# Two groups of TensorE products in a linear attention layer, ordered by their contraction rows

## What is computed

```python
GLA_HEADS = 4; GLA_DK = 192; GLA_DV = 384; GLA_CHUNK = 16

def step(s, inp):                       # one chunk of the recurrence, all in float32
    qc, kc, vc, ac = inp
    bc = jnp.cumsum(ac, axis=2)         # the logarithm of the decay since the chunk's start
    o_inter = jnp.einsum('bhcd,bhde->bhce', qc * jnp.exp(bc), s)
    diff = bc[:, :, :, None, :] - bc[:, :, None, :, :]
    decay = jnp.exp(jnp.where(tril[:, :, None], diff, -jnp.inf))
    att = jnp.einsum('bhid,bhjd,bhijd->bhij', qc, kc, decay)
    o_intra = jnp.einsum('bhij,bhje->bhie', att, vc)
    last = bc[:, :, -1:, :]
    s_new = (jnp.exp(last[:, :, 0, :, None]) * s
             + jnp.einsum('bhcd,bhce->bhde', kc * jnp.exp(last - bc), vc))
    return s_new, o_inter + o_intra
```

## Time and profile before

| | us |
|---|---|
| median of 3 runs | 3801.09 |
| the 3 runs | 3800.23 to 3805.05 |
| the profiled execution, its own time | 3801.69 |
| its span in the trace | 3799.4 |
| PE busy | 3385.1 (89% of the span) |
| mean granted clock of TensorE | 0.909 of full speed |
| `score_levels`, from PE's first product to its last mask | 2479.1 to 2572.1 |
| the 8 sampled sequences of `linear_outputs` | 2601.6 to 2711.7 |

### The profile page before, as it was taken

How to read it: one execution, slowest core, us unless ns; L and a number is a source line. 1 busy time by engine, 2 the same in 40 slices (tenths; PEclk the granted TensorE clock), 3 DMA queues, 4 the chain that set the end, 5 groups by cost and what they waited for, 6 DMA issues and landing times. The chain is left out here.

```text
span 3799.4 us, 57145 instructions
## 1 busy us (share of the span) xinstructions
PE 3385.1 (89%) x23817; PEld 3082.7 (81%) x23817; DVE 1640.8 (43%) x1879; ACT 1274.2 (34%) x1363; POOL 208.7 (5%) x131
## 2 busy tenths in 40 slices
PE   7799999676567999999999999899659999999999
PEld 5699999354245999999999999763249999999999
DVE  4543334444554454333443444344444543334333
ACT  3432323123465343323333333230143433333322
POOL 0000000001231000000000000052010000000000
PEclk9899999656788999999999999957769999999999
DMA  4545352302564445454545444203235454445454
GB/s 145 184 159 174 118 158 86 122 1 89 178 200 134 156 156 166 145 166 157 165 155 165 153 161 166 74 1 128 88 140 166 147 163 154 164 158 164 146 166 136
DMA packets 317204, 537.06 MB, mean 141 GB/s; under 512 B 18213, under 2 KB 115455, under 8 KB 316040
## 3 DMA queue, kind: packets, MB, share of 16 engines
q1 hardware_dynamic: 316376, 529.70, 42.5%
q10 hardware_dynamic: 624, 4.46, 0.3%
HBM read 517.23 MB, written 25.19 MB: 143 GB/s over the span
## 5 line engine op out<-in xcount | busy, mean ns | idle before, releaser
L468 DVE TENSOR_TENSOR project_weights_low<-ring,project_weights_high 128x2048 fp32r<-128x2048 f32 x344 | 788.5, 2292 | 1201.9 <-ACT project_weights_high L403 1201.9
L403 ACT ACTIVATE project_weights_high<-ring 128x2048 fp32r<-128x2048 f32 x344 | 658.6, 1915 | 1263.3 <-PE project_banks L333 1263.2
L331 PE MATMUL project_banks<-high,project_weights_high 128*128 128x288 f32 x2560 | 763.9, 298 | 45.4 <-DVE project_weights_low L458 41.1
L332 PE MATMUL project_banks<-low,project_weights_high 128*128 128x288 f32 x2560 | 762.2, 298 | 0.0
L333 PE MATMUL project_banks<-high,project_weights_low 128*128 128x288 f32 x2560 | 761.8, 298 | 0.0
L331 PE MATMUL project_banks<-up_high,project_weights_high 128*128 128x288 f32 x2048 | 610.6, 298 | 27.5 <-DVE project_weights_low L458 27.5
L332 PE MATMUL project_banks<-up_low,project_weights_high 128*128 128x288 f32 x2048 | 609.6, 298 | 0.0
L333 PE MATMUL project_banks<-up_high,project_weights_low 128*128 128x288 f32 x2048 | 609.3, 298 | 0.0
L331 PEld LDWEIGHTS project_banks<-high,project_weights_high 128*128 128x128 f32 x2560 | 488.3, 191 | 48.1 <-DVE project_weights_low L458 42.6
L332 PEld LDWEIGHTS project_banks<-low,project_weights_high 128*128 128x128 f32 x2560 | 488.0, 191 | 0.0
L333 PEld LDWEIGHTS project_banks<-high,project_weights_low 128*128 128x128 f32 x2560 | 486.9, 190 | 0.0
(11 more groups left out here) (422 smaller groups left out, 3336.9 us busy)
## 6 DMA issues: line engine op xcount, KB each, us to landing
ring<-in_w_up_dram SPq DMA_DIRECT2D x128, 1024.0 KB, 5.2
ring<-in_w_down_dram SPq DMA_DIRECT2D x128, 1024.0 KB, 5.1
ring<-in_gla_w_in_dram SPq DMA_DIRECT2D x40, 1024.0 KB, 4.9
h<-in_cache_nsa_kv_dram SPq DMA_DIRECT2D x256, 128.0 KB, 2.1
ring<-in_w_out_dram SPq DMA_DIRECT2D x32, 1024.0 KB, 5.1
ring<-in_nsa_w_in_dram SPq DMA_DIRECT2D x28, 1024.0 KB, 5.0
sp_keys_values<-in_cache_nsa_kv_dram SPq DMA_DIRECT2D x80, 256.0 KB, 3.5
ring<-in_w_mem_kv_dram SPq DMA_DIRECT2D x16, 1024.0 KB, 5.3
```

Source lines behind the costliest of these rows:

```text
L331: nc.tensor.matmul(bank, w_high, moving_high[:, kt], start=(kt == 0), stop=False)
L332: nc.tensor.matmul(bank, w_high, moving_low[:, kt], start=False, stop=False)
L403: nc.scalar.activation(weights_high[:, c % 2], g.ring[:, c % RING], ACT.Copy).then_inc(rounded, 1)
L468: nc.vector.tensor_tensor(weights_low[:, c % 2], g.ring[:, c % RING], weights_high[:, c % 2].bitcast(F32), ALU.subtract).then_inc(split, 1)
```

## The change

The order of the products on PE is changed in two places, and nothing else. In `score_levels`, where a level took head after head with both of its pieces, it now takes all 128-row pieces of the level (span by span, the four heads in each) and then all 64-row pieces. A PSUM bank now gets its first piece marked as the start of the accumulation once, at the first span, and the products skip the check of groups. In `linear_outputs` the few products take the 128-row pieces of the four heads and then the 64-row pieces. The number of products, their operands and the semaphores on which each engine waits are the same.

```diff
@@ score_levels, PE's list
-                for h in range(GLA_HEADS):
+                for rows_used in (P, P // 2):
                     for keys, queries, col in spans:
                         n = keys.stop - keys.start
-                        pieces = head_pieces(h)
-                        for e, (t, rows) in enumerate(pieces):
+                        for h in range(GLA_HEADS):
+                            t, rows = next(x for x in head_pieces(h) if x[1].stop - x[1].start == rows_used)
+
                             mm = nc.tensor.matmul(ps[0:n, level % 2, h, col:col + n], lk[rows, t, keys],
-                                                  lq[rows, t, queries], start=(e == 0), stop=(e == len(pieces) - 1))
+                                                  lq[rows, t, queries], start=(rows_used == P and col == spans[0][2]),
+                                                  stop=(rows_used < P), skip_group_check=True)
                 mm.then_inc(scored, 1)
@@ linear_outputs, PE's list
-                    for e in range(2):
+                    for rows_used in (P, P // 2):
                         for h in range(GLA_HEADS):
-                            t, rows = head_pieces(h)[e]
+                            t, rows = next(x for x in head_pieces(h) if x[1].stop - x[1].start == rows_used)
                             mm = nc.tensor.matmul(few_ps[32 * h:32 * h + 32, 0:GLA_DV], own_q[rows, half, t],
                                                   before[rows, half, t], start=False,
-                                                  stop=(last and half == 1 and e == 1), skip_group_check=True)
+                                                  stop=(last and half == 1 and rows_used < P), skip_group_check=True)
```

## The result

The changed kernel takes 3771.9 us (median of 4 runs, 3770.2 to 3773.6) against 3801.7 us for the kernel before (4 runs): a ratio of 0.992, with a 95% interval of 0.9903 to 0.9938. That is 30 us less. The forecast was 39 us less, 3762 us; the range of 3747 to 3784 held the time. The profiled execution has a span of 3768.0 us, 31.4 us less than before.

The account below looks back on a forecast made before the run. The prediction took PE to set both blocks by its shares, with a POOL and DVE ring equally long in the middle levels. Levels 9.8 plus loop 29 gave 39 us off 3801.1: 3762 us, range 3747 to 3784.

Parts of the forecast that it names:

- What an order costs: PE at 1.2 GHz: 0.31 us per change of height; two 64-row products in opposite halves for the price of one.
- The ring in the levels: Score levels: POOL's keys, DVE's diff and mask, POOL's add, 10.14 us without PE; levels 3 to 6 gain 0.
- the upper bound: Score levels: CROSS on a 2.4 GHz clock is 1.4 us shorter, so 11.2 us saved instead of 9.8.
- the lower bound: Score levels: one more DVE instruction of 1.8 us beside POOL's last keys leaves 8.0 us saved.
- f: Sampled loop: time of one sequence's few products, 1.5 us at 2.4 GHz or 2.8 at 1.2, instead of 8.1.
- third rival: Few products: 64-row pieces don't overlap in one bank, some 3 us more a sequence; 3786 us, chance 0.04.
- the third case: Sampled loop: clock where it is now, few products slow and states fast; 8.7 us a sequence, 35.7 us saved.
- the case of all at 1.2 GHz: Sampled loop, second case: few products and states at 1.2 GHz; 11.9 us a sequence, 9.5 us saved.
- The loop's term: Sampled loop: 29 us saved (9.5 to 42.8), with 9.5 us taken for a sequence.
- the first rival: Sampled loop: short bursts don't raise the clock, states and few products run at 1.2 GHz; 3782 us, chance 0.16.
- What is late next: Sampled loop: the old state's load holds two sequences to at least f + 14.6 us, 8.1 to 8.7 us each.
- Everything else: Outside both blocks: nothing gained or lost, no DMA, wait or instruction moved on another queue.

Follow-up runs that it names:

- e3: The changed kernel with the states' products over 128 contraction rows instead of 32, the added rows zeros: 3756.0 us, ratio 0.9879 to the kernel before.
- e7: e3 with SP issuing the load of the next old state before the store of the new one: 3749.9 us, ratio 0.9868 to the kernel before.
- e1: The kernel before with only the score levels in the changed order, few products as before: 3793.4 us, ratio 0.9973.
- e4: e3 with the few products in the order of before, levels as changed: 3769.7 us, ratio 0.9919 to the kernel before.
- e2: The kernel before with only the few products in the changed order, score levels as before: 3782.8 us, ratio 0.9949.
- e5: The changed kernel with mask(level) before diff(level + 3) on DVE's list in the score levels: 3762.4 us, ratio 0.9899 to the kernel before.

## Why the prediction was right, and where it was off

- **What an order costs** held: 0.31 us a change of height; a level of 16 products at 5.4 us forecast and 4.8 to 5.6 measured, 5.38 in level 4, whose last pairs already ran at 2.4 GHz; two 64-row products at the price of one, also in four pairs in a row.
- **The ring in the levels** held: PE lost half of its work, and levels 3 to 6 gained nothing. Levels 1 and 2 came forward by 14.29 - 10.77 = 3.5 and 13.51 - 10.77 = 2.7 us from `diff` to `diff` (3.42 and 2.66 forecast). The end of the block gained 4.5 us instead of 3.7: CROSS took 1.80 us and not 2.8, the case of the upper bound, a clock of 2.4 GHz. What the lower bound allowed for came too, but cost nothing: POOL's last keys but one took 4.93 us instead of 3.42 beside DVE's queries, and the add behind them, now without DVE beside it, took 2.35 instead of 3.79. Sum 10.7 for 9.8 (8 to 11.2).
- **The few products** held: f was put at 1.5 or 2.8 us and measured at 1.6 and 2.9 us, and the bank was no hindrance (third rival).
- **The step that was off is the length of a sequence:** "I take 9.5 us for a sequence, nearer to the third case than to the second". Five of the seven are 11.82 us, which is the case of all at 1.2 GHz (11.9 us), and only the first two (6.6 and 9.4 us) were faster; the first is even below the 8.1 us named as the least. The loop's term was 29 us and measured 20.5. The reason given for the choice was that the clock rises within every row of few products now. That was true of few products of 8 us; the step from them to bursts of 2.9 us wasn't covered by any row. What remained after the change is mostly states, and the rows already showed the clock down again behind 5.4 us of states (0.94 us for a pass of the last tile, and a clock of 0.50 from the next few product on the earlier trace rows).
- **The number was helped by luck.** 3772 us lies midway between the forecast of 3762 and the first rival's 3782 ("The clock stays down", chance 0.16), and the range held both. The trace decides between them, and it decides for the rival from the third sequence on; its size was too pessimistic by some 11 us in the loop, since the first two sequences and the states of the last ran wholly or partly at 2.4 GHz. Its reason, that short bursts don't raise the clock, holds only beside states of 32 contraction rows: in e3 the same short bursts go with a clock of 0.90.
- **What is late next** was named rightly, the load, but with the clock down it isn't reached: one wait of 0.28 us. e3 shows it, with waits of 2.4 to 3.0 us and 8.8 us a sequence on average (from 2592.13 to 2653.75 in seven), for 8.1 to 8.7 forecast.
- **Everything else** at nothing: 0.2 us more in each of the two stretches behind the levels and the loop, 0.6 us less ahead of the levels, where nothing was changed.

## What to carry to other kernels

Products that use only part of the array should stand beside others of the same height and with other columns or other rows: here four of 32 columns, or two of 64 rows in opposite halves, take the time of one, also into one bank. A change of height costs 0.31 us at 1.2 GHz in the levels and 0.15 in the few products. Before halving an engine's work in a block, follow the rings of waits in which it doesn't stand, since they decide how much of it comes back. And where the work taken away is what kept TensorE's clock up, cost the rest at the lower clock as well, and try whether the rest can be put on more contraction rows at the same column count.

## What was not expected of the hardware

The clock fell and stayed at 1.2 GHz with PE busy for 64.5 of 64.8 us, when most of the products had 32 contraction rows, and stayed at 2.4 GHz for the most part when the same columns were streamed over 128 rows with zeros in 96 of them (0.58 in the changed kernel's loop, 0.90 in e3's, 1.00 in e7's; with the old order of the few products 0.77 in e1's and 1.00 in e4's). The Trainium skill (TensorE: Matmul & The Clock Gate, Loop structure matters more than you think) ties a warm clock to matmuls that stay back to back. These were back to back, and the measurement says that this wasn't enough. The levels say so too: with the heights alternating PE was busy for 91.8 of 93.4 us at a clock of 0.51, and with them grouped for 44.2 of 82.7 us at 0.69, though no product's rows changed there. What the clock goes by in the levels wasn't tested. Why the states of the sixth and seventh sequence were faster in e2 and e5, and those of the last in the changed kernel, stays open.

DVE and POOL hinder each other, in both directions. POOL's add of 1024 elements a partition takes 2.35 us with DVE idle (the last add of the levels, in the kernel before and in the changed one) and 3.79 where DVE's queries begin just ahead of it. `diff` takes 1.76 us alone and 3.9 where POOL's add begins just ahead of it, and the add then keeps its 2.35: whichever begins second waits for the other. DVE's mask and POOL's keys don't show it (1.21 and 3.43 us beside each other in e5).
